# Attention values with V as the stationary operand, softmax factors applied before the turn, and one PSUM bank per query tile

## The reference

```python
# NSA (branch C): three attentions on the same queries, gated and added
o = gb[..., 0:1] * o_c + gb[..., 1:2] * o_s + gb[..., 2:3] * o_w
# DSA (branch A): 64 best keys by an indexer, then
p = masked_softmax(s, (sel <= t[None, :, None])[:, None])
return jnp.einsum('bhqk,bqkd->bqhd', p.astype(vg.dtype), vg)
# merge of the branches, then the output projection
sum_b sigmoid(g_b) * (y_b @ proj_b)
```

## Time and profile before

| | |
|---|---|
| median of three runs | 1286.19 us |
| the three runs | 1284.16, 1286.19, 1292.02 us |
| span of the profiled execution, first to last instruction | 1282.8 us |
| median less that span | 3.4 us |
| TensorE busy | 1261.5 us, 98% |
| VectorE busy | 765.9 us, 60% |
| ScalarE busy | 637.8 us, 50% |
| DMA | 220.98 MB, 172 GB/s on average |

### The profile page before, as it was taken

How to read it: one execution, slowest core, us unless ns; L and a number is a source line. 1 busy time by engine, 2 the same in 40 slices (tenths; PEclk the granted TensorE clock), 3 DMA queues, 4 the chain that set the end, 5 groups by cost and what they waited for, 6 DMA issues and landing times.

```text
span 1282.8 us, 18946 instructions
## 1 busy us (share of the span) xinstructions
PE 1261.5 (98%) x6244; PEld 1042.6 (81%) x6244; DVE 765.9 (60%) x1466; ACT 637.8 (50%) x1079; POOL 71.7 (6%) x147
## 2 busy tenths in 40 slices
PE   7999999999999999999999999999999999999996
PEld 6888888888888888888878888888888888888885
DVE  5555557546766775555575555564567586655555
ACT  5444446556655364444364444464666544444442
POOL 4300001500000000000000000034000000000000
PEclk9999999999999999999999999999999999999998
DMA  8654454533233455555455555444232344654543
GB/s 335 228 180 178 173 188 140 208 121 132 100 132 132 176 178 185 196 196 193 169 220 178 194 196 196 171 158 172 101 130 103 128 164 151 224 180 179 196 175 136
DMA packets 31599, 220.98 MB, mean 172 GB/s; under 512 B 3504, under 2 KB 4144, under 8 KB 5552
## 3 DMA queue, kind: packets, MB, share of 16 engines
q1 hardware_dynamic: 30384, 214.60, 46.4%
q10 hardware_dynamic: 1120, 5.57, 1.3%
q0 software_dynamic: 32, 0.00, 0.0%
HBM read 218.58 MB, written 1.05 MB: 171 GB/s over the span
## 4 chain that ended last, share of the span: by engine, by line
PE 98%; DMA 1%; DVE 1%; issue 0%; DVEq 0%; ACT 0%; ACTq 0%; SPq 0%
PE G L1225 23%; PE G L1227 22%; PE G L1226 22%; PE O L1225 3%; PE SC L1226 3%; PE O L1226 3%; PE SC L1225 3%; PE SC L1227 3%; PE O L1227 3%; PE O L1453 3%; PE T L1398 3%; PE SC L1408 2%; PE T L1302 1%; PE T L1502 1%; PE T L1241 1%; DMA raw<-stream 1%
## 5 line engine op out<-in xcount | busy, mean ns | idle before, releaser
L835 DVE TENSOR_TENSOR wlo<-raw,whi 128x1024 fp32r<-128x1024 f32 x398 | 471.2, 1226 | 296.4 <-ACT whi L503 294.8
L503 ACT ACTIVATE whi<-raw 128x1024 fp32r<-128x1024 f32 x398 | 399.2, 1053 | 273.8 <-PE G L1227 145.7
L1225 PE MATMUL G<-whi,xhi 128*128 128x512 f32 (+1 forms) x1216 | 482.4, 397 | 6.8 <-DVE xlo L859 6.8
L1227 PE MATMUL G<-whi,xlo 128*128 128x512 f32 (+1 forms) x1216 | 472.4, 389 | 0.0
L1226 PE MATMUL G<-wlo,xhi 128*128 128x512 f32 (+1 forms) x1216 | 471.5, 388 | 0.0
L1225 PEld LDWEIGHTS G<-whi,xhi 128*128 128x128 f32 x1216 | 229.5, 189 | 55.5 <-DVE xlo L859 7.5
L1227 PEld LDWEIGHTS G<-whi,xlo 128*128 128x128 f32 x1216 | 229.3, 189 | 48.1
L1226 PEld LDWEIGHTS G<-wlo,xhi 128*128 128x128 f32 x1216 | 229.9, 189 | 43.8
L561 ACT ACTIVATE shared_q<-G,stat 128x256 f32<-128x256 f32 x88 | 41.8, 475 | 169.8 <-PE G L1227 167.4
L904 DVE SCALAR_TENSOR_TENSOR shared_q<-shared_q,G 128x256 f32<-128x256 f32 x88 | 36.6, 416 | 98.9 <-ACT shared_q L561 98.9
L655 ACT ACTIVATE probs<-sm,stat 128x256 f32<-128x256 f32 (+2 forms) x128 | 51.9, 406 | 53.0 <-DVE stat L1029 53.0
(11 more groups left out here) (162 smaller groups left out, 1017.4 us busy)
## 6 DMA issues: line engine op xcount, KB each, us to landing
raw<-stream SPq DMA_DIRECT2D x201, 1024.0 KB, 4.8
gates<-w_in ACTq DMA_DIRECT2D x2, 2048.0 KB, 9.4
x<-x_in SPq DMA_DIRECT2D x2, 512.0 KB, 7.5
out<-x SPq DMA_DIRECT2D x4, 256.0 KB, 2.1
small<-small_in ACTq DMA_DIRECT2D x2, 414.5 KB, 3.1
const<-const_in SPq DMA_DIRECT2D x1, 689.0 KB, 14.0
z<-final_in SPq DMA_DIRECT2D x1, 512.0 KB, 3.7
kvcT<-kvcT ACTq DMA_DIRECT2D x2, 255.0 KB, 4.0
```

Source lines behind the costliest of these rows:

```text
L503: act.activation(whi[s][:, c : c + PART], raw[s][:, c : c + PART], ACT.Copy).then_inc(hi_done, 1)
L835: dve.tensor_tensor(wlo[s][:, c], raw[s][:, c], whi[s][:, c].bitcast(F32), ALU.subtract).then_inc(lo_done, 1)
L1225: pe.matmul(o, ahi, bhi, start=first, stop=False)
L1227: return pe.matmul(o, alo, bhi, start=False, stop=last)
```

## The change: what it does

- The values are formed transposed. V (64 columns) is the stationary operand, the turned probabilities of two heads (256 columns, 512 for cmp) the moving one, and the result, 64 channels x queries, goes to the lower or the upper 64 partitions of a bank by the head's parity. A `qt` 1 batch has 4 such products, a `qt` 0 batch 2, a cmp batch 2 of 512 columns.
- Since the queries are now columns, the softmax factor can't be applied to the result. `weigh` takes the place of `drain_o`: it multiplies `probs` by the factor before the turn, and `batch_turn` waits for it (`weighed`) and no more for `exp_done`. `probs` has two buffers.
- All kinds of one query tile add up in one bank, O[qt]. The batches are ordered by query tile: sel, sel, win, win, cmp of tile 0, those of tile 1, then dsa.
- `y` and its four turns (16 transposes a layer) go. `split_o` splits the bank itself, into `ychi`/`yclo` for NSA and `xhi`/`xlo` for DSA.

```diff
-BATCHES = (
-    [("sel", qt, g) for qt in range(2) for g in range(2)]
...
+def _nsa(qt):
+    return [("sel", qt, 0), ("sel", qt, 1), ("win", qt, 0), ("win", qt, 1), ("cmp", qt, 0)]
...
+BATCHES = _nsa(0) + _nsa(1) + [("dsa", qt, g) for qt in range(2) for g in range(2)]
...
-        probs = sb("probs", [P, 1024])
+        probs = [sb("probs0", [P, 1024]), sb("probs1", [P, 1024])]
...
+                def split_o(branch, tok, dst, ks):
+
+                    act.wait_ge(values_done, l * NB + BANK_END[branch, tok])
+                    act.activation(
+                        dst[:, ks : ks + 4, tok * P : (tok + 1) * P],
+                        O[tok][:, :].rearrange("p (k t) -> p k t", k=4), ACT.Copy,
+                    ).then_inc(t_hi_done, 1)
...
-                    dve.wait_ge(o_filled, l * NB + b + 1)
-                    src = O[b % 2][:, 0 : nh * HD].rearrange("p (h d) -> p h d", d=HD)
...
-                        dve.tensor_tensor(dst, src, fb, ALU.mult).then_inc(o_drained, 1)
...
-                        ins = dve.tensor_tensor(dst, dst, tmp, ALU.add)
...
+                    p = probs[b % 2][:, 0 : nh * w].rearrange("p (h k) -> p h k", k=w)[:, :, 0:n]
+                    dve.tensor_tensor(p, p, f.unsqueeze(2).to_broadcast([P, nh, n]), ALU.mult).then_inc(weighed, 1)
...
+                weigh(0)
                 mask_and_max(1)
                 split(l, at, 13)
                 for k in range(12):
                     c, tok = Z_CHUNKS + k // 2, k % 2
                     if tok:
                         split(l, at, 2 * c + 2)
-                    drain_o(k)
+                    weigh(k + 1)
+                    if k in (5, 10):
+                        split_o(3 + k // 10, k // 10, ychi, yclo, 0)
...
-                for j in range(2):
-                    split_y(f"yc{j}", 3 + j, xhi, xlo, 0)
+                weigh(13)
+                split_o(5, 0, xhi, xlo, 4)
                 gated(0, 1, 0, 0)
...
-                    pe.wait_ge(exp_done, l * NB + b + 1)
+                    pe.wait_ge(weighed, l * NB + b + 1)
...
-                            ins = pe.matmul(O[b % 2][:, hh * HD : (hh + 1) * HD], lhs, rhs, start=kb == 0, stop=last)
-                    ins.then_inc(o_filled, 1)
+                            p = pT[:, 4 * kb + 2 * grp : 4 * kb + 2 * grp + 2, :].rearrange("p h q -> p (h q)")
+                            ins = pe.matmul(
+                                O[qt][rows, 256 * g : 256 * (g + 1)], v, p, start=opens and kb == 0,
+                                stop=kind == "dsa" and kb == qt, skip_group_check=True)
+                    ins.then_inc(values_done, 1)
```

More of the change, by code:

```diff
@@ L253, in trunk @@
         exp_done = sem("exp_done")
+        weighed = sem("weighed")
         roped = sem("roped")
@@ L776, in mixer @@
                         split(l, at, 2 * c + 3)
-                for j in range(2):
-                    split_y(f"yc{j}", xhi, 0)
+                split_o("dsa", 0, xhi, 4)
                 split(l, at, 26)
@@ L781, in mixer @@
                 split(l, at, 27)
+                split_o("dsa", 1, xhi, 4)
                 split(l, at, 28)
-                for j in range(2):
-                    split_y(f"ya{j}", xhi, 4)
                 split(l, at, 29)
@@ L1029, in mask_and_max, with weigh @@
                     dve.tensor_scalar(negmax[:, 0:nh], rowmax[:, 0:nh], -0.125, None, ALU.mult).then_inc(negmax_done, 1)
-                def drain_o(b):
+                def weigh(b):
                     kind, qt, g = BATCHES[b]
-                    nh = heads_of(b)
+                    n, nh = keys_of(b), heads_of(b)
+                    w = 16 if kind == "cmp" else n
                     f = fac[:, 0:nh]
@@ L1154, in mixer @@
                 split(l, at, 27)
-                drain_o(13)
+                split_o(6, 1, xhi, xlo, 4)
                 gated(1, 2, 0, 0)
@@ L1158, in mixer @@
                 split(l, at, 28)
-                for j in range(2):
-                    split_y(f"ya{j}", 5 + j, xhi, xlo, 4)
                 gated(1, 2, 1, 0)
@@ L1437, in batch_values @@
                     kind, qt, g = BATCHES[b]
-                    if b >= 2:
-                        pe.wait_ge(o_drained, l * NB + b - 1)
+                    opens = g == 0 and kind in ("sel", "dsa")
+                    if opens and b >= 10:
+                        pe.wait_ge(o_drained, l * 4 + qt + 1)
                     wait_drained(pe, l, *turn_names(b))
-                    for j, name in enumerate(turn_names(b)):
-                        for n, (hh, kb) in enumerate(turns_of(b)[j]):
-                            grp = hh % 2
+                    for kb in range(1 if kind == "cmp" else qt + 1):
+                        for grp in range(2):
+                            rows = slice(grp * HD, (grp + 1) * HD)
```

94 lines of the change are left out of this document (39 added, 55 removed).

## The result

The changed kernel takes 1316.85 us (median of 4 runs, 1315.43 to 1319.16) against 1286.4 us (median of 4, 1284.16 to 1292.02) for the kernel before. The ratio is 1.0244, with a 95% interval of 1.0215 to 1.0273: slower by 2.4%. The forecast was 1316.0.

A forecast was written before the change was run, and what follows sets the result against it. TensorE's program bounded the kernel; the new wait on the weighing adds +13.6 +1.4 -0.9 = +14.1 us a layer, +28.2 for two. 1282.8 + 28.2 + 3.4 = 1314.4, clock +1.8: 1316 us, range 1303 to 1338.

The forecast's parts named there:

- the main saving on TensorE: Shorter value products, hidden in the new wait in the slots: worth 0.7 us a layer of the 7 it has.
- about 122 us: The loop of 12 slots in a layer: 122.3 us after the change against 108.7 before, +13.6 a layer.
- The wake-up: TensorE resuming after each wait in the loop: 0.07 us each by an estimate, 0.84 a layer.
- about 50 us in total: Sign: TensorE's transposes of `probs` have some 28 waits on the weighing, 0.7 to 2.7 us each.
- The chain: Each slot, scores through mask, exponentials, rounding and subtraction to weighing: 7.3 to 9.8 us, together 101.2 a layer.
- The clock term: Falls of TensorE's clock after waits: two a layer at 1 us, less 1.1 for each of two old falls: +1.8.
- the text's own last test: Sign: if the granted clock is low in more than four stretches, the forecast's clock term is wrong.
- Ahead of and behind the loop: Work before the 12 slots of a layer, +1.4 us, and after them, -0.9 us.
- The 3.4: Time around the profiled span, added to 1311.0 us of span to give 1314.4.
- TensorE's work decides: Rival: the waits are hidden and cheaper value products and dropped turns show, 1267.5 us, or 1273 with tiling changes; chance 0.08.
- The values one after the other: Rival: value products run in series and the wait is short, 1291 us, no change; chance 0.06.
- The clock falls in most slots: Rival: half of the 24 slots pay turn and scores again, 20 us, giving 1335; chance 0.14.

The follow-up runs named there:

- experiment 1: The changed kernel with each weighing moved on VectorE ahead of the `wlo` pair, behind the mask: 1270.21 us, ratio 0.9863.
- experiment 9: The kernel before, with the weighing added behind the `wlo` pair and the turn waiting for it, O scaled twice: 1325.5 us, ratio 1.0293.
- experiment 10: The kernel before, with the weighing added ahead of the `wlo` pair and the turn waiting for it: 1286.2 us, ratio 0.9998.
- experiment 4: The changed kernel with every product of the values issued twice: 1317.51 us.
- experiment 5: The version of experiment 1 with every product of the values issued twice: 1286.9 us, ratio 1.0002.
- experiment 7: The changed kernel with the value products in the old form (turned probabilities stationary, 64 columns of V moving): 1320.57 us.
- experiment 6: The version of experiment 1 with the value products in the old form (turned probabilities stationary): 1284.66 us, ratio 0.9986.
- experiment 11: The version of experiment 1 with all value products written to one column half, partitions 0 to 63: 1288.17 us, ratio 1.0005.
- experiment 2: The changed kernel with the multiply of `probs` replaced by a nop, the wait and its place kept: 1289.08 us, ratio 1.0014.
- experiment 8: The version of experiment 1 with the value products ordered all of one column half, then all of the other: 1270.65 us, ratio 0.9875.
- experiment 3: The changed kernel without the multiply of `probs`, the turn waiting only for the exponentials: 1270.69 us, ratio 0.9866.

## Why the prediction was right

**The mechanism.** "So the turn now waits for scores, mask, exponentials, a weight unit's rounding, its subtraction, and the weighing": experiments 1, 9 and 10 show it from both sides. The 46.6 us between the changed kernel and experiment 1 come of the weighing's place alone, and the wait alone makes the kernel before slow. That "the main saving on TensorE" is hidden is shown by 4 against 5 and by 7 against 6. The multiply's 1.23 us, taken from an operation of the same size, measured 1.22; the 0.69 for 512 elements measured 0.69. Values of tile 1 at 1.06 us for four products measured 1.01. Their working side by side, which the prediction took from the scores, is shown by experiment 11. The loop was put at "about 122 us" and took 122.98 and 124.01; TensorE's busy share, put near 95%, is 96%. The wake-up, put at 0.07 us without a row, is 0.06 in slot 6 (354.27 to 354.33). One sign did not come as it was written: for "about 50 us in total" of waits in some 28 turns, the matmuls' row has 34.8 us in 25. The prediction put the falls of the clock beside the waits, but a fall in a chunk or in the values makes TensorE arrive later and shortens the wait behind it. The idle 34.8 and the 13.0 us of slower work together are 47.8.

**The terms of the sum.** The parts of the first layer's loop, from the starts of its turns and scores, are these:

| part | predicted | measured |
|---|---|---|
| scores' end to turn, 12 slots | 102.0 | 100.3 |
| turns and scores | 20.3 | 22.7 |
| loop | 122.3 | 123.0 |

The predicted column holds no fall of the clock, the measured one does. Both parts are off, and they cancel in part. The chain was too long mostly in its `cmp` batches: slot 8 was put at 8.3, with the wake-up 8.37; that turn came 7.72 us behind the scores' end. VectorE's mask of the 8 heads in that slot:

```profile
368.26 0.17 DVE L1031 CUSTOM_DVE_ANT_0 sm<-SC,const 128x15 f32<-128x15 f32 x1 [2.20 <-issue]
...
369.12 0.17 DVE L1037 TENSOR_SCALAR stat<-stat 128x8 f32<-128x8 f32 x1
...
375.02 0.19 DVE L1046 RECIPROCAL fac<-stat 128x8 f32<-128x8 f32 x1
```

The slot starts at 368.13. The mask is through 1.16 us later, without a pause; the reciprocal comes at S + 6.89. In the kernel before the same mask began at S + 0.28, paused for 0.3 us in its middle, ran at a wider step, and was through at S + 1.86, so its reciprocal stood at S + 7.58: the 0.7 that the estimate has too much. Slot 3, the other `cmp` batch, was 0.8 below for the same reason and a smaller delay by pooling. The other slots were off by at most 0.5 either way, the largest, slot 10, by a fall in its chunk. The other part was too short, and for one reason mostly: the clock. In slot 4 turn and scores took 3.31 us in place of 2.03, in slot 6 2.63; that is 1.9 of the 2.4 us. The remaining 0.5 are the turns: 0.58 us for tile 0, where "half of 0.97" was put, and 1.02 for tile 1, where the earlier trace rows gives 0.97.

**The clock term was the one mis-sized.** "I take two a layer at 1 us, 4 us, less 1.1 for each of the two falls there are now": there were eight falls, not four. By the lengths of their slots against slots of the same kind without one, they cost 1.3, 0.6, 0.45, 0.45, 1.5, 1.0, 0.55 and 0.55, about 6.4 us, 0.8 each, where 4 were forecast. The size of one was right: dear where it meets turn and scores, cheap where it lies in a chunk ahead of a wait. The number was not. Taking off 1.1 for each of the two falls of before was a slip of the sum: the 108.7 us of the old loop, which is taken off already, holds its fall, and the chain of 122.3 was built from rows without one. A fall of before also costs more than 1.1, since TensorE waits for nobody there: the one at 372 us also stretched the scores from 0.65 to 1.10 us (371.42 to 372.52), and the one at 1003 us made its chunk 7.22 us long where 5.60 is usual. By the text's own last test ("if the granted clock is low in more than four stretches, the clock term is" wrong) this one failed.

Each of the eight falls begins in or within 2 us behind a wait of TensorE. Six of them belong to the seven longest waits on the weighing (1.95 to 2.34 us), two to the other 18. In experiments 4, 7 and 9 the tie is looser: five of the eight waits of about 2 us have a fall behind them. A wait makes a fall likelier and no more. The clearest case is the wait for `xlo` at the start of the second layer, which every kernel here has. The row behind it in the kernel before, whose window at 644 us the prediction read as a sign against falls, and then in experiment 1, with a window of 1 us:

```profile
645.78 0.50 PE L1225 MATMUL G<-whi,xhi 128*128 128x512 f32 x1 [3.08 <-DVE xlo L859]
```

```profile
638.05 0.50 PE L1230 MATMUL G<-whi,xhi 128*128 128x512 f32 x1 [2.94 <-DVE xlo L867]
...
639.00:640.00 1.00, 1.00 (x4) 0.72 (x4) 1.00 (x5) 1.00 (x2) 0.00 (x0) 0.50 0.00 0
```

That wait is 2.8 to 3.2 us long in all 13 profiled executions. The clock falls behind it in nine of them and stays up in four (before, the changed kernel, experiments 2 and 5). One execution's row could not tell.

The Trainium skill, "TensorE: Matmul & The Clock Gate", Part 1, has the throttled clock as the default, released by activity. The runs lean that way more than the prediction did, with 8 falls in this kernel and 11 in experiment 9, but do not follow it simply: experiment 2 keeps 23 waits of up to 1.1 us, and its profiled execution has no fall.

**Ahead of and behind the loop.** +1.4 and -0.9 a layer were put; the starts of the same chunks in both traces give +1.35 (without a drift of 0.6 us that the first layer had by then) and about -0.6. The time around the span was 1.8 us, not 3.4. The 3.4 was never that time: it was a median less the span of another execution, and wherever both are known for one execution of the kernel before they differ by 2.1 to 2.2 us. So the sum against the execution before is 1282.8 + 31.4 + 1.8 = 1316.0, and the forecast's 1282.8 + 28.2 + 1.8 + 3.4 = 1316.2: the span grew 1.4 us more than forecast, and the margin around it shrank by 1.6. Larger errors cancel inside the span. Without their falls the two loops are about 120.6 and 120.0 us where 122.3 was put, 4.0 us too much in the sum; the falls then brought 6.4 us where the net term had 1.8, 4.6 too little. The mechanism and the range were earned; that the number hit is luck.

**The rivals.** "TensorE's work decides" put 1267.5 for the case that VectorE weighs before the pair; that case was then built, and took 1270.21. For the changes of form the prediction had 5.6 us by an estimate from the earlier trace rows (1273), beside the Trainium skill, "TensorEngine Tiling (Array Packing)", Key Properties, by which a change of tiling mode drains the engine. That is an upper end: 2.7 us are left between the sum without it and the run, and the starts of the rows give 0.13 us a batch (experiment 6), 3.6 us for 28. "The values one after the other" is 1288.17 in experiment 11, where 1291 had been put. "The clock falls in most slots" did not come in this kernel, with eight falls in or next to its 24 slots, most of them cheap; experiment 9 comes nearest to it.

## What to carry to other kernels

When a step is put into a loop that one engine starts and waits for again, its price is not its duration but its place in the other engine's program: here 28 weighings cost nothing ahead of a pair of subtractions that nobody was in a hurry for, and 46.6 us behind it, a part of that by the clock, which fell more often once TensorE waited. So read from the timeline when the operand of the new step is ready and what stands between that moment and the step; if a slot's chain becomes longer than the bounding engine's own work, move the step before judging the change. And a saving on the engine that bounds a kernel is only worth what the waits leave of it: double that work once, and see whether the time moves.

## What was not expected of the hardware

- Products whose outputs go to different column halves overlap in TensorE even if they are not neighbours in the program: a tile-1 batch takes 1.0 us in either order (experiments 1 and 8) and 1.9 us if all go to one half (experiment 11).
- The clock falls are more frequent where TensorE waits for the weighing: eight, six and eleven in the profiled executions of the changed kernel and of experiments 7 and 9 (two of the six in experiment 7 of double length), none to three in those without such a wait (experiments 1, 3, 5, 6, 8, 10, 11 and the kernel before). Yet they don't follow the idle time alone: experiment 4, with 22.3 us of such waits, had four, and experiment 2, with 16.8, none. In the changed kernel one costs from 0.45 to 1.5 us by where it lands, and in the kernel before, where nothing hides it, about 1.6. These are counts of one execution each, and other executions of a kernel differ: experiment 5 took 1285.3 to 1285.9 us in five executions, at a mean granted clock of 0.996, and 1287.9 to 1288.9 in the other five, at 0.992 to 0.993. What sets one off was not found.
- The clock also falls without any idle time, and in these runs only behind the old `cmp` products. The kernel before and experiments 6 and 10 have two such falls each, one in each layer, all in the scores or the first chunk product that follow sixteen records of this form; one fall of experiment 9, at 1031 us, is of the same kind. The five kernels with V stationary and no wait in the loop (experiments 1, 3, 5, 8, 11) have none in their loops. From slot 9 of the kernel before, just ahead of the fall of the earlier trace rows:

```profile
368.91 1.99 PE L1453 MATMUL O<-ikd,pT 15*128 15x64 f32 x16
```

- The weight loads pause where the form of the products changes, though nobody is waited for. In experiment 1 it is this row of the waits, 0.35 us a batch, mostly hidden behind the products that still run:

```profile
PEld O L1464 <- issue: 8.5, 24, 0.4
```
